# Recurrent heads with state products inside the gate stream, a rounded spread of the gate rows, an earlier first feed-forward turn, and query tiles in another place

## The reference

```
for i in (0, 1):
    hn = rmsnorm(x, norm_mix_w[i])
    x = x + (mlstm_mixer(hn, ...) if i == 0 else window_attn_mixer(hn, ...))
    x = x + (silu(g) * u) @ ffn_w_out[i]        # g, u = rmsnorm(x) @ ffn_w_in[i]
# mlstm_chunkwise, for one direction (the other runs on flipped rows), b = cumsum(log_f):
kv_chunk = einsum('bhcl,bhcld,bhcle->bhcde', w, k, v)       # state of a chunk
s   = einsum(q, k) * exp(D - m_t),  D = b_t - b_s + log_i (lower triangle)
num = s @ v + inter * (q @ C_prev);   den = sum(s) + inter * (q . n_prev)
h   = num / max(|den|, exp(-m_t));   then a norm over each head, times sigmoid(o)
```

## Time and profile before

| | us |
|---|---|
| runs | 1025.29, 1028.20, 1029.03 |
| profiled execution | 1030.92 |
| its span | 1028.9 |
| TensorE busy | 974.7 |
| VectorE busy | 589.2 |
| ScalarE busy | 480.5 |
| POOL busy | 24.0 |

### The profile page before, as it was taken

How to read it: one execution, slowest core, us unless ns; L and a number is a source line. 1 busy time by engine, 2 the same in 40 slices (tenths; PEclk the granted TensorE clock), 3 DMA queues, 4 the chain that set the end, 5 groups by cost and what they waited for, 6 DMA issues and landing times.

```text
span 1028.9 us, 14249 instructions
## 1 busy us (share of the span) xinstructions
PE 974.7 (95%) x5267; PEld 816.8 (79%) x5267; DVE 589.2 (57%) x1096; ACT 480.5 (47%) x762; POOL 24.0 (2%) x39
## 2 busy tenths in 40 slices
PE   6999799899999989999999999989899999999996
PEld 6876587688888889887888888878898888888875
DVE  4854757553546577457454545764764456555665
ACT  5554446344444346546353535564433344444442
POOL 0002200000000000000000000000000000000000
PEclk9999999899999999899999999999999999999999
DMA  5651245445454522235535364312432234333441
GB/s 207 242 200 46 82 166 182 161 148 219 147 220 149 199 104 83 82 121 205 223 144 229 138 229 163 141 42 103 172 110 82 81 124 149 125 123 124 143 164 41
DMA packets 25349, 149.49 MB, mean 145 GB/s; under 512 B 2992, under 2 KB 3120, under 8 KB 11088
## 3 DMA queue, kind: packets, MB, share of 16 engines
q1 hardware_dynamic: 24624, 146.39, 39.0%
q0 software_dynamic: 672, 2.38, 0.7%
HBM read 147.71 MB, written 1.05 MB: 145 GB/s over the span
## 4 chain that ended last, share of the span: by engine, by line
PE 78%; DVE 9%; ACT 5%; DMA 3%; issue 2%; DVEq 2%; SPq 0%; ACTq 0%
PE bank L427 22%; PE bank L428 21%; PE bank L429 21%; DMA w_raw<-w_main_dram 3%; DVE w_lo L1633 2%; PE bank L486 2%; DVE w_lo L1547 1%; ACT w_hi L1135 1%; PE bank L812 1%; ACT w_hi L1080 1%; PE bank L932 1%; DVEq L1960 1%; PE bank L673 1%; PE bank L799 1%; PE bank L947 1%
## 5 line engine op out<-in xcount | busy, mean ns | idle before, releaser
L427 PE MATMUL bank<-w_hi,x_hi 128*128 128x512 f32 (+2 forms) x664 | 267.3, 403 | 1.8 <-DVE ffn_nat L1856 1.3
L428 PE MATMUL bank<-w_lo,x_hi 128*128 128x512 f32 (+2 forms) x664 | 260.1, 392 | 0.0
L429 PE MATMUL bank<-w_hi,x_lo 128*128 128x512 f32 (+2 forms) x664 | 258.5, 389 | 0.0
L1547 DVE TENSOR_TENSOR w_lo<-w_raw,w_hi 128x2048 fp32r<-128x2048 f32 x56 | 126.8, 2289 | 48.1 <-ACT w_hi L1080 47.9
L427 PEld LDWEIGHTS bank<-w_hi,x_hi 128*128 128x128 f32 x664 | 125.3, 189 | 31.3 <-issue 4.3
L429 PEld LDWEIGHTS bank<-w_hi,x_lo 128*128 128x128 f32 x664 | 124.7, 188 | 27.9
L428 PEld LDWEIGHTS bank<-w_lo,x_hi 128*128 128x128 f32 x664 | 125.0, 188 | 23.1
L1633 DVE TENSOR_TENSOR w_lo<-w_raw,w_hi 128x2048 fp32r<-128x2048 f32 x46 | 105.2, 2290 | 50.9 <-ACT w_hi L1135 50.8
L1080 ACT ACTIVATE w_hi<-w_raw 128x2048 fp32r<-128x2048 f32 x58 | 109.6, 1912 | 43.0 <-DMA w_raw<-w_main_dram 36.3
L1135 ACT ACTIVATE w_hi<-w_raw 128x2048 fp32r<-128x2048 f32 x46 | 87.3, 1907 | 16.9 <-PE bank L429 12.3
L1856 DVE SCALAR_TENSOR_TENSOR ffn_nat<-bank,stat,ffn_nat 128x256 f32<-128x256 f32 x44 | 21.1, 482 | 124.7 <-ACT ffn_nat L1266 124.6
(11 more groups left out here) (326 smaller groups left out, 1525.7 us busy)
## 6 DMA issues: line engine op xcount, KB each, us to landing
w_raw<-w_main_dram SPq DMA_DIRECT2D x111, 1024.0 KB, 4.9
s_raw<-w_side_dram SPq DMA_DIRECT2D x51, 512.0 KB, 4.1
h<-x_dram SPq DMA_DIRECT2D x2, 512.0 KB, 4.7
w_raw<-w_main_dram SPq DMA_DIRECT2D x2, 512.0 KB, 7.5
arena<-rows_dram POOLq DMA_DIRECT2D x2, 512.0 KB, 3.9
out_dram<-arena SPq DMA_DIRECT2D x1, 512.0 KB, 2.6
out_dram<-arena SPq DMA_DIRECT2D x2, 256.0 KB, 2.1
arena<-c_l_dram POOLq DMA_DIRECT2D x1, 384.0 KB, 6.0
```

Source lines behind the costliest of these rows:

```text
L427: pe.matmul(out, ah, bh, start=first, stop=False)
L428: pe.matmul(out, ah, bl, start=False, stop=False)
L429: return pe.matmul(out, al, bh, start=False, stop=last)
L1547: dve.tensor_tensor(w_lo[:, slot, 4 * g:4 * g + 4, :], w_raw[:, g, :, :], w_hi[:, slot, 4 * g:4 * g + 4, :], ALU.subtract).then_inc(w_lo_o ...
```

## The change

- A head's gate tile is issued in three parts, and the two state products stand between them. VectorE instead of ScalarE copies the states into m_c, behind sd_ok.
- The spread takes rows that VectorE has split into a rounded part and its rest, on partitions 0 to 3 and 32 to 35 of n_hl and i_hl, which lie in g_hi and g_lo. One fp32r matmul each, with a broadcast column of row_sel as weights, replaces the fp32 products with m_sel. POOL clears the rows; of the first constant only the mask is loaded.
- Chunks 5 and 6 are split and completed in halves, one in each head, ahead of the norms.
- The parameters are loaded ahead of x.
- In both feed-forwards ScalarE's and VectorE's part of the first turn comes ahead of chunk c0 + 2. The angles are computed in block 2 and the meta rows' norm in block 9, between the products of the two row blocks. On both engines blocks 1 and 2 are taken out of the loop.
- In attention the whole of query tile 2 follows the first scores, and the halves of tile 3 follow the scores of the next two groups. The split of half 0 of chunk 23 moves from head 9 to head 7.

```diff
@@ -116,7 +116,7 @@
 OUT_PARTS = ((0, slice(0, D)), (1, slice(0, CH)), (1, slice(CH, D)))
-A_HALVES = {0: (C_AOUT, 0), 4: (C_AOUT, 1), 9: (C_AOUT + 1, 0)}
+A_HALVES = {0: (C_AOUT, 0), 4: (C_AOUT, 1), 7: (C_AOUT + 1, 0)}
@@ -219,7 +219,7 @@
         m_mask = l0c[:, 0:2 * P].rearrange("p (a b) -> p a b", a=2)
-        m_sel = l0c[:, 2 * P:].rearrange("p (a b) -> p a b", a=H0)
+        n_hl, i_hl, row_sel = g_hi[:, 0:2 * S], g_lo[:, 0:2 * P], g_lo[:, 2 * P:2 * P + H0]
         g_rows = ar(11152, 4, S)
@@ -329,9 +329,9 @@
             sp.dma_start(ident[:, :], ident_d).then_inc(in_landed, 16)
+            sp.dma_start(par[:, :], params).then_inc(in_landed, 16)
             for r in range(R):
                 sp.dma_start(h[:, r, :], x_d[r * P:(r + 1) * P, :]).then_inc(x_landed[r], 16)
-            sp.dma_start(par[:, :], params).then_inc(in_landed, 16)
             first = w_raw[:, 0, :, :].rearrange("p k n -> p (k n)")
@@ -377,9 +377,11 @@
             pool.memset(row_1[0:H0, :, :], 1.0)
+            pool.memset(n_hl[0:36, :].bitcast(F32), 0.0)
+            pool.memset(i_hl[0:36, :].bitcast(F32), 0.0)
             pool.memset(v_aug[:, :, :, DV:DV + 1], 1.0)
             pool.memset(v_aug[:, :, :, DV + 1:VW], 0.0).then_inc(va_ok, 1)
-            pool.dma_start(l0c, c_l0).then_inc(c0_landed, 16)
+            pool.dma_start(l0c[:, 0:2 * P], c_l0[:, 0:2 * P]).then_inc(c0_landed, 16)
@@ -580,16 +582,15 @@
-            pe.wait_ge(c0_landed, 16)
+            pe.wait_ge(hl_ok, 1)
             for hh in range(H0):
...
                     pe.wait_ge(ei_ok, hh)
-                pe.matmul(bank[3][:, :], m_sel[0:H0, hh, :], row_n[0:H0, :, :].rearrange("p a b -> p (a b)"),
-                          start=True, stop=True).then_inc(bc_ps, 1)
-                pe.matmul(bank[2][:, 0:2 * P], m_sel[0:H0, hh, :], row_i[0:H0, :, :].rearrange("p a b -> p (a b)"),
-                          start=True, stop=True).then_inc(in_ps, 1)
+                select = row_sel[0:36, hh:hh + 1].to_broadcast([36, P])
+                pe.matmul(bank[3][:, :], select, n_hl[0:36, :], start=True, stop=True).then_inc(bc_ps, 1)
+                pe.matmul(bank[2][:, 0:2 * P], select, i_hl[0:36, :], start=True, stop=True).then_inc(in_ps, 1)
@@ -600,8 +601,8 @@
-                part_a(C_MO + hh // 2, ("mo", hh // 2, hh % 2), hh % 2, 0, KT)
-
+                gate_part = lambda k0, k1: part_a(C_MO + hh // 2, ("mo", hh // 2, hh % 2), hh % 2, k0, k1)
+                gate_part(0, 4)
                 for d in range(2):
@@ -611,6 +612,7 @@
                     pe.matmul(bank[5][:, 0:VW], m_kw[:, d, :], v_aug[:, d, hh, :], start=True, stop=True).then_inc(c_ps, 1)
+                    gate_part(4 + 2 * d, 6 + 2 * d)
                 pe.wait_ge(sd_ok, hh + 1)
@@ -827,7 +829,7 @@
             a_scores(0)
-            a_queries(2, 0, KT // 2)
+            a_queries(2, 0, KT)
             for j in range(NG):
@@ -836,15 +838,13 @@
                 if j < 2:
-                    a_queries(2 + j, (1 - j) * KT // 2, (2 - j) * KT // 2)
+                    a_queries(3, j * KT // 2, (j + 1) * KT // 2)
                 if j == NG - 1:
...
                     a_values(n + i - 1)
-                    if (j, i) == (1, 1):
-                        a_queries(3, KT // 2, KT)
                     if j == NG - 1 and i < NG - 1:
@@ -1174,7 +1174,9 @@
                     else:
-                        carry(v_aug[:, r, 2 * c:2 * c + 2, 0:DV], ("mv", c, r), scale=stat[:, 24 + r:25 + r])
+                        key = ("mv", c, r)
+                        act.activation(v_aug[:, r, 2 * c:2 * c + 2, 0:DV], acc_in(key)[:, :], ACT.Copy,
+                                       scale=stat[:, 24 + r:25 + r]).then_inc(acc_free[USE[key] % 2], 1)
             act.wait_ge(mc_ps, 1)
@@ -1201,18 +1203,11 @@
                     squares(hh - 1)
-                if hh == 2:
-                    split_main(C_MO + 2, 0)
+                split_half(C_MO + 1 + hh // 2, 1 - hh // 2, hh % 2)
                 key = ("mo", hh // 2, hh % 2)
...
                                      scale=half_0[:, hh % 2:hh % 2 + 1]), key)
-                for d in range(2):
-                    n = 2 * hh + d
-                    act.wait_ge(c_ps, n + 1)
-                    if hh:
-                        act.wait_ge(n_ps, 4 * hh)
-                    act.activation(m_c[:, d, :], bank[5][:, 0:VW], ACT.Copy).then_inc(c_ok, 1)
                 for r in range(R):
@@ -1271,8 +1266,9 @@
-                def block_(f, j, last=False):
-                    turned(f - 1)
+                def block_(f, j, last=False, first=False):
+                    if not first:
+                        turned(f - 1)
                     gate(f)
@@ -1291,12 +1287,15 @@
                     split_side(u0 + s)
+                turned(0)
                 split_main(c0 + 2, c0 % 2)
+                block_(1, 1, first=True)
                 if layer == 0:
...
                     act.activation(um[0:M, :], hm[0:M, :], ACT.Square, accum_out=stat[0:M, 0:1]).then_inc(ss_ok, 1)
-                with act.Fori(0, (FB - 1) // 2 - 1) as i:
+                block_(2, 2)
+                with act.Fori(1, (FB - 1) // 2 - 1) as i:
                     block_(2 * i + 1, 1)
@@ -1717,7 +1716,16 @@
             ins.then_inc(rows_ok, 1)
-            for c in range(3, C_MO + 2):
+            dve.tensor_tensor(row_sel, ident[:, 0:H0], ident[:, 32:32 + H0], ALU.add)
+            dve.drain()
+            ri = row_i[0:H0, :, :]
+            n_part, i_part = (lambda p, t=t: t[p:p + H0, :].rearrange("p (a b) -> p a b", a=2) for t in (n_hl, i_hl))
+            dve.tensor_copy(n_part(0), rn)
+            dve.tensor_copy(i_part(0), ri)
+            dve.drain()
+            dve.tensor_tensor(n_part(32), rn, n_part(0), ALU.subtract)
+            dve.tensor_tensor(i_part(32), ri, i_part(0), ALU.subtract).then_inc(hl_ok, 1)
+            for c in range(3, C_MO + 1):
                 rest_main(c, c % 2)
@@ -1750,8 +1758,10 @@
                 ins.then_inc(sd_ok, 1)
-                if hh == 2:
-                    rest_main(C_MO + 2, 0)
+                for d in range(2):
+                    dve.wait_ge(c_ps, 2 * hh + d + 1)
+                    dve.tensor_copy(m_c[:, d, :], bank[5][:, 0:VW]).then_inc(c_ok, 1)
+                rest_half(C_MO + 1 + hh // 2, 1 - hh // 2, hh % 2)
                 if hh == H0 - 1:
@@ -1846,11 +1856,17 @@
+            def meta_rows():
+                rstd("meta", [(1, D)], rows=M, out=28)
+                dve.tensor_scalar(um[0:M, :], hm[0:M, :], stat[0:M, 28:29], None, ALU.mult).then_inc(um_ok, 1)
+
             def ffn(layer, first_tiles, after):
...
-                def product(f):
+                def product(f, between=None):
                     for r in range(R):
+                        if r and between is not None:
+                            between()
                         b_ = (n0 + r) % 2
@@ -1861,9 +1877,10 @@
-                def block_(f, j, last=False):
-                    turned(f - 1)
-                    product(f)
+                def block_(f, j, last=False, first=False, between=None):
+                    if not first:
+                        turned(f - 1)
+                    product(f, between)
                     if not last:
@@ -1879,16 +1896,14 @@
                     rest_side(u0 + s)
+                turned(0)
                 rest_main(c0 + 2, c0 % 2)
-                if layer == 0:
-                    angles()
-                with dve.Fori(0, (FB - 1) // 2 - 1) as i:
+                block_(1, 1, first=True)
+                block_(2, 2, between=angles if layer == 0 else None)
+                with dve.Fori(1, (FB - 1) // 2 - 1) as i:
                     block_(2 * i + 1, 1)
                     block_(2 * i + 2, 2)
-                if layer == 0:
-                    rstd("meta", [(1, D)], rows=M, out=28)
-                    dve.tensor_scalar(um[0:M, :], hm[0:M, :], stat[0:M, 28:29], None, ALU.mult).then_inc(um_ok, 1)
-                block_(FB - 2, 1)
+                block_(FB - 2, 1, between=meta_rows if layer == 0 else None)
                 block_(FB - 1, 2, last=True)
...
```

More of the change, by code:

```diff
@@ L294, in two_blocks @@
         block = ctx.enter_context(nc.Block())
-        gr_ok, fa_ok, fe_ok, rows_ok, mc_ps, mc_ok = (sem(n) for n in ("gr_ok", "fa_ok", "fe_ok", "rows_ok", "mc_ps", "mc_ok"))
+        gr_ok, fa_ok, fe_ok, rows_ok, hl_ok, mc_ps, mc_ok = (sem(n) for n in ("gr_ok", "fa_ok", "fe_ok", "rows_ok", "hl_ok", "mc_ps", "mc_ok"))
         kn_ps, kn_ok, bc_ps, t_ok, in_ps, ei_ok = (sem(n) for n in ("kn_ps", "kn_ok", "bc_ps", "t_ok", "in_ps", "ei_ok"))
```

## The result

The changed kernel takes 1012.51 us, the median of four runs (1012.23 to 1012.83), against 1026.74 us (1023.22 to 1029.03) of the kernel before beside it. The ratio of the runs is 0.9846, 95% interval 0.9819 to 0.9873. Forecast were 1014.1 us and 1006 to 1022. On a second chip the changed kernel took 1012.69 and the kernel before 1028.68 us (0.9842, 0.9824 to 0.9859). The profiled execution took 1012.64 us, with a span of 1010.9 us.

The account below looks back on a forecast made before the run. TensorE was taken as the bound, busy 974.7 of 1028.9 us, so only its waits and low clock counted. Terms 0.3 - 0.7 + 7.3 + 0.7 + 6.5 = 14.1 us took the median from 1028.2 to 1014.1, range 1006 to 1022.

Parts of the forecast that it names:

- Start: Kernel start: parameters ahead of x and a shorter constant load gain 0.3 us (bounds 0.4 lost to 1.1 gained).
- Stall at chunk 3: Before the heads: VectorE's added spread instructions make TensorE stand 1.3 us before chunk 3.
- Spread: Heads: time freed by the rounded spread turns into the wait for ScalarE's bank reading; 0 of 4.5 us gained.
- Head period: Recurrent heads: VectorE's queue gives a period of 11.8 us; head 3's norms at 117.7 against 118.54, 0.8 us gained.
- Idle of TensorE: Recurrent heads: TensorE idles about 1.9 us a head and some 7 us behind head 3.
- Low clock in the heads: Recurrent heads: one stretch of 3.4 us at 1.2 GHz, taken as costing 1.5 us.
- Heads as a whole: Recurrent heads: 0.7 us lost in all (bounds 6 gained to 6 lost).
- First turn: Both feed-forwards: the earlier first turn removes TensorE's wait for the low half; 7.3 us gained in layer 0, 0.7 in layer 1.
- rival 4: Feed-forward: low half early, but the next tile waits for chunk 10, so the 5.33 us only move; 1021.4, chance 0.03.
- Attention: Attention loop: moved query tiles and split remove TensorE's waits and low clock; 6.5 us gained (bounds 2.5 and 9.3).
- Rival 2: Attention: ScalarE paces the loop or the clock falls elsewhere; gain 1.0 instead of 6.5, time 1019.6, chance 0.2.
- Rivals 1 and 3: Heads: half chunk hides, 10.1 us a head, 1009, chance 0.14; or 1.2 GHz through all heads, 1036.6, chance 0.03.

Follow-up runs that it names:

- the last experiment: e_early_root with VectorE's five spread instructions moved from ahead of chunk 3's rest to behind it; 1005.32 us, 0.9769 of the kernel before.
- heads: The kernel before with only the start and heads parts of the change; 1027.82 us, 0.9996 of the kernel before.
- e_early: The changed kernel with VectorE's half-chunk rests moved ahead of the state-decay product in heads 1 to 3; 1008.68 us, 0.9797 of the kernel before.
- e_early_root: e_early with two root steps of the first normalisation placed between head 3's state copies; 1006.90 us, 0.9798 of the kernel before.
- e_warm128: The changed kernel with 22 unread products of 128 rows in TensorE's idle of head 3; 1012.97 us, 0.9851 of the kernel before.
- e_warm: The changed kernel with 22 unread products of 36 rows in TensorE's idle of head 3; 1012.38 us, 0.9836 of the kernel before.
- e_nospread: The changed kernel with the old fp32 spread, the whole constant load and no split rows on VectorE; 1015.19 us, 0.9861 of the kernel before.
- e_behind: The changed kernel with each head's half-chunk rest behind that head's norms instead of ahead; 1012.23 us, 0.9849 of the kernel before.

## Why the prediction was right

- **Start**, 0.3 us forecast. The first product begins at 10.79 us instead of 11.18: 0.39 us.
- **Stall at chunk 3**, 1.3 us: measured 1.15, and the last experiment shows its cause.
- **Spread**, 0 of 4.5 us. Some 0.4 us a head by the one clean period, 1.2 to 1.6 us in all; the wait for ScalarE took most of the rest. The forecast of nothing was too low, and the run without it is 1.5 to 2.7 us longer, low clock included.
- **Head period**, 11.8 us and norms at 77.3, 89.1, 100.9, 117.7. Measured: scores 68.25, 79.79, 91.29, 103.17, so 11.5, 11.5 and 11.9 us; norms of head 0 at 76.78, of head 2 at 99.83, of head 3 at 118.22; head 3's normalisation at 113.07 (112.7). Head 3's scores come 6.8 us earlier than in the earlier trace rows, and its norms 0.3 us: head 3 gives the gain back, as the prediction said. The 0.5 us between 117.7 and 118.22 are two misses that offset each other: 117.7 holds no low clock, and without it the norms start at 116.82 ("heads"). Of head 3's queue e_early shows the half chunk's part. The larger one was argued only: the normalisation ran beside the gate tile before, and now stands behind the state copies that VectorE has taken over; e_early_root moved two of its steps, 1.2 us.
- **Idle of TensorE**, 1.9 us a head and some 7 behind head 3. Measured, before the last value products and the next scores together, 0.9 to 1.3 us in heads 0 to 2, and 5.4 to 5.8 in head 3. The period was near all the same, as it was worked out along VectorE's queue.
- **Low clock in the heads**, one stretch of 3.4 us for 1.5 us. One such stretch came (104.0 to 107.4 us); head 2's norms to head 3's take 18.39 us with it and 16.83 in e_warm128 without it: 1.56. The second, 10.2 us behind head 3, was not in the sum and cost little (0.36 us for 6.8 us more of it). The kernel before had two stretches of 3.4 us of its own in this part (78 to 82 and 129 to 133 us), which the prediction's list leaves out.
- **Heads as a whole**, 0.7 us lost: 1.45 gained in the pair of profiles; with the start 0.4 by the ratio of the timed runs (2.4 gained to 1.5 lost). The sign is within the spread, so this term is neither confirmed nor refuted.
- **First turn**, 7.3 and 0.7 us: 7.44 and 0.95, and 7.65 for the part alone (8.0 by the sum). Chunk 10 fits, which ends rival 4.
- **Attention**, 6.5 us: 6.58 in the traces, 4.0 for the part alone in the medians, and 4.0 against the attention of "heads". Rival 2 (1.0 us) is out, but the term is likely sized by the low clock of one execution (4.8 of its 9.6 us are such time). The 2.2 us left idle were 0.53 and 1.16 and some shorter ones.
- **Rivals 1 and 3.** No head of 10.1 us; the clock didn't stay low through the heads.
- **POOL and VectorE**, up to 2.4 us by the rule on the port. The POOL pass of 0.6 us stands in no rows; in the traces it is the key scaling (0.60). In the changed kernel VectorE's half chunks took 2.28 us in every head, so nothing of the 2.4 came.

The mechanisms named were right: the early turn, the waits of attention, VectorE's queue in head 3. That the total came within 1.6 us of 1014.1 is in part luck: the parts alone add up to 12.5 us in the medians, attention below its term, and the whole to 14.2 to 16.0.

The step with least ground was the sum's last one: the profiled execution stood 2.7 us over the first median, taken off as if both kernels had that distance. Runs of the changed kernel lie within 0.6 and 1.9 us on two chips, those of the kernel before within 8.9 (23 runs on one: 1023.82 to 1032.68, with mean clocks from 0.991 to 0.981): its low stretches come and go from run to run, and a distance to the median is no property of the change.

## What to carry to other kernels

Where an engine's queue is the path, put its fixed work into the time in which that same engine waits for another: the same 2.28 us were free ahead of the state-decay product, paid in full in head 3 ahead of the normalisation, and behind the norms they only moved the wait. Price a stretch at the lower clock only where the other engines wait for TensorE. Small instructions that make a saving possible have a place too: five of them cost 1.15 us until they stood behind chunk 3's rest. And before a low stretch of one profile goes into a sum, look how long the same, unchanged code takes in another execution.

## What the runs showed of the hardware

- Products of 36 rows, 22 in a row with no gap, did not keep the granted clock at 2.4 GHz (fall at 116.4 us); those of 128 rows did, in the same place, until 126 us. The Trainium skill (TensorE: Matmul & The Clock Gate, Part 1) has the gate follow how busy TensorE has been lately; by that rule both should hold. The trace of e_warm disagrees: busy 10.00 of 10.00 us with a mean clock of 0.92. This is one trace of each, and e_warm's had a fall at 102 to 107 us that the other's had not, so they differ before the products begin; the mean clocks of five runs each (0.989 to 0.993, and 0.994 to 0.995) point the same way. Whether it is the rows or the data in them was not tried.
- TensorE's clock fell at 104.0 us with no idle above 1.17 us in the 12 us ahead of it, and at 699.6 us in the kernel before but not in the changed one, for the same instructions. The kernel of e_nospread, whose waits in heads 0 to 2 are all under 0.5 us, had three stretches of 3.4 us between 80 and 112 us. A profile of one execution can't tell such a stretch from a property of the kernel.
- POOL's gate pass took 1.82 us beside the end of VectorE's half chunk (99.26 and 112.70 us), against 1.50 and 3.42 in the earlier trace rows, and VectorE's pass stayed at 2.28. It is not always POOL alone that pays: in e_behind, where the half chunk meets POOL's scaling of the queries, VectorE's took 2.48, 2.48 and 2.57 us, and the POOL pair beside it 2.92 instead of 0.88:

```profile
90.99 2.92 POOL L399 TENSOR_TENSOR arena<-arena 128x128 f32<-128x128 f32 x2 [0.64 <-ACT arena L1197]
91.12 2.48 DVE L1632 TENSOR_TENSOR w_lo<-w_raw,w_hi 128x2048 fp32r<-128x2048 f32 x1
```
